# Expert stage in two lanes of 64 rows, each with its own expert, on the two column halves of the array

## What is computed

```
flat = expert.reshape(-1)
counts = jnp.bincount(flat, length=N_EXPERTS)
...
return (jax.nn.silu(xb @ w_eg[e]) * (xb @ w_eu[e])) @ w_ed[e]
...
y = jnp.einsum('nk,nkd->nd', gate.astype(t.dtype), y)
```

## Time and profile before

| | us |
|---|---|
| median of 3 runs | 2869.02 |
| lowest and highest | 2868.82, 2869.57 |
| the profiled execution | 2867.73 |
| its span in the trace | 2866.1 |
| first gate matmul of the expert stage to the first transfer of the stage behind it | 1717.1 to 2818.0 |

### The profile page before, as it was taken

One profiled execution on the slowest core, in us unless ns is written; L12 is line 12 of the kernel. 1 busy time (PEld: TensorE's weight loads), 2 busy tenths in 40 slices (PEclk: granted clock), 3 DMA queues, 4 the chain that ended last, 5 costly groups with the idle time before them and its releaser, 6 DMA issues. The chain is left out here.

```text
span 2866.1 us, 28552 instructions
## 1 busy us (share of the span) xinstructions
PE 2592.7 (90%) x7895; PEld 1293.1 (45%) x7896; DVE 854.1 (30%) x2231; ACT 498.1 (17%) x982; POOL 697.3 (24%) x582
## 2 busy tenths in 40 slices
PE   5797999999995896999999939999999999999990
PEld 2344444444442473455555524444444444444440
DVE  0136665757578111233333330110011010101103
ACT  1121222222211122222222101111111111111112
POOL 0024645555464000011111111111111111211114
PEclk9898999999997998999999969999999999999995
DMA  7120111010104115322111136677756784645966
GB/s 279 59 99 26 42 47 55 33 55 33 59 30 176 54 76 212 117 74 74 59 59 59 59 116 214 193 248 230 261 180 228 244 290 132 223 143 188 340 211 264
DMA packets 153556, 397.15 MB, mean 139 GB/s; under 512 B 18498, under 2 KB 19034, under 8 KB 153482
## 3 DMA queue, kind: packets, MB, share of 16 engines
q1 hardware_dynamic: 125533, 338.28, 32.7%
q0 software_dynamic: 18336, 51.53, 7.5%
q10 hardware_dynamic: 9621, 6.51, 0.8%
HBM read 326.16 MB, written 70.35 MB: 138 GB/s over the span
## 5 line engine op out<-in xcount | busy, mean ns | idle before, releaser
L773 PE MATMUL a_psz<-W 128*128 128x512 f32 x1088 | 484.6, 599 | 1.3 <-ACT W L585 1.3
L671 DVE SCALAR_TENSOR_TENSOR yacc<-aext,pcol,yacc 128x256 f32<-128x256 f32 x928 | 369.9, 477 | 0.0
L1838 PE MATMUL e_psg<-W,e_xT 128*128 x784 | 346.4, 595 | 2.0 <-DVE e_xT L1797 2.0
L1859 PE MATMUL e_psy<-W,e_hT 128*128 x784 | 344.7, 593 | 1.0 <-ACT e_hT L1770 1.0
L1842 PE MATMUL e_psu<-W,e_xT 128*128 x784 | 344.5, 593 | 0.0
L773 PEld LDWEIGHTS a_psz<-W 128*128 128x128 f32 x1088 | 205.7, 193 | 239.2 <-issue 239.2
L555 POOL TENSOR_TENSOR a_vn<-a_vn,gv 128x512 f32<-128x512 f32 x17 | 243.1, 14303 | 15.2 <-ACT a_vn L619 15.2
L1544 PE MATMUL r_psx<-W 128*128 128x512 f32 x544 | 238.1, 596 | 0.0
L1842 PEld LDWEIGHTS e_psu<-W,e_xT 128*128 128x128 f32 x784 | 149.3, 190 | 187.2 <-issue 187.2
L1803 DVE TENSOR_TENSOR e_hb<-e_psu,e_sg 128x512 f32<-128x512 f32 x49 | 33.9, 692 | 661.4 <-PE e_psu L1842 352.8
L1518 PE MATMUL r_pss<-W,r_h2T 128*128 128x512 f32 x512 | 227.5, 598 | 1.4 <-DVE r_h2T L1390 1.4
(11 more groups left out here) (276 smaller groups left out, 2193.1 us busy)
## 6 DMA issues: line engine op xcount, KB each, us to landing
W<-in_w_expert_gate SPq DMA_DIRECT2D x32, 2048.0 KB, 12.9
W<-in_w_expert_up SPq DMA_DIRECT2D x32, 2048.0 KB, 18.2
W<-in_w_expert_down SPq DMA_DIRECT2D x32, 2048.0 KB, 22.4
W<-in_x_prompt SPq DMA_DIRECT2D x32, 512.0 KB, 3.9
x_scratch<-W SPq DMA_DIRECT2D x17, 512.0 KB, 2.9
r_x1r<-x_scratch SPq DMA_DIRECT2D x17, 512.0 KB, 4.3
x_scratch<-r_x SPq DMA_DIRECT2D x17, 512.0 KB, 2.9
h_scratch<-r_h SPq DMA_DIRECT2D x17, 512.0 KB, 2.9
```

Of the source, the lines that this page charges most:

```text
L671: ins = dve.scalar_tensor_tensor(out=out, in0=src, scalar=w, in1=yacc[:, i, :], op0=ALU.mult, op1=ALU.add)
L773: last = pe.matmul(psz[bank][:], hT[t.par][:, k, :], w_in[:, k, COL[bank]:COL[bank] + 512], start=(k == 0), stop=(k == KD - 1))
L1838: last = pe.matmul(psg[:], xT[t.par][:, k, :], W[:, bass.ds(base + 512 * k, 512)], start=(k == 0), stop=(k == KD - 1))
L1859: last = pe.matmul(psy[:, 512 * n:512 * n + 512], hT[:, k, :], W[:, bass.ds(base + 8192 + 1024 * k + 512 * n, 512)], start=(k == 0), stop= ...
```

## The change

The 128 rows of a step become two lanes of 64 rows. Lane 0 works through the experts 0 to 15, lane 1 through the experts 16 to 31, each with blocks of up to 64 pairs of its own expert. Each matmul of 128 rows becomes two of 64 rows (`both`), one into the partitions 0 to 63 of the result and one into 64 to 127, which is on the two column halves of the array. Lane 1 has one slot of `W`, lane 0 the two others by turns; gate, up and down have a semaphore each, and a part of an expert can be loaded as soon as that part of the expert before is done. The order of the loads is sorted on the chip. The planning stage is gone, and its work is done at the start of the expert stage, with the list of steps turned by PE into rows. On PE, a step now ends what it begins: gate_up of this step, then the transposes of the next step's tokens and this step's hidden rows by turns, then down of this step. The bound of the loop is `STEPS_MAX`, 83, where `NBMAX` was 65.

```
-NBMAX = (PAIRS - NE) // P + NE
+LANES = 2
+HALF = P // LANES
+EPL = NE // LANES
+REG = CAP + HALF
+STEPS_MIN = PAIRS // P
+STEPS_MAX = (PAIRS - EPL) // HALF + EPL
...
-        def load_part(eng, e, slot, n):
-            base = W[:, EXPERT_COLS * slot + 4096 * n:EXPERT_COLS * slot + 4096 * n + 4096]
-            name, k, here = (("w_expert_gate", KD, gate_up_here), ("w_expert_up", KD, gate_up_here), ("w_expert_down", KE, down_here))[n]
-            eng.dma_start(base.rearrange("p (k n) -> p k n", k=k),
+        def load_part(eng, e, base, n, r):
+            name, k, here = (("w_expert_gate", KD, gate_here), ("w_expert_up", KD, up_here), ("w_expert_down", KE, down_here))[n]
+            need(eng, here, 16 * r)
+            if not isinstance(r, int):
+                settle(eng)
+            dst = W[:, base + 4096 * n:base + 4096 * n + 4096] if isinstance(base, int) else W[:, bass.ds(base + 4096 * n, 4096)]
+            eng.dma_start(dst.rearrange("p (k n) -> p k n", k=k),
                           I[name][0][bass.ds(e, 1), :, :].rearrange("a (k p) n -> p (a k) n", p=P)).then_inc(here, 16)
-        def load_expert(eng, e, slot):
-            need(eng, gate_up_here, 32 * e)
-            for n in range(2):
-                load_part(eng, e, slot, n)
-            need(eng, down_here, 16 * e)
-            load_part(eng, e, slot, 2)
...
-            def count_blocks(eng):
-                return eng.value_load(ends[0:1, NE - 1:NE], min_val=PAIRS // P, max_val=NBMAX)
-            def block_steps(eng, nb, parts):
+            def count_steps(eng):
+                eng.wait_ge(S["count_known"], 1)
+                return eng.value_load(count[0:1, 0:1], min_val=STEPS_MIN, max_val=STEPS_MAX)
+            def expert_steps(eng, ns, parts):
                 def step(b):
                     for k, work in parts:
                         t = b.at(k)
-                        if isinstance(t.v, int):
-                            if 0 <= t.v < PAIRS // P:
-                                work(t)
-                                continue
-                            if t.v < 0:
-                                continue
-                        with eng.If(t.v < nb):
+                        if isinstance(t.v, int) and t.v < STEPS_MIN:
                             work(t)
-                steps(eng, step, 4, (NBMAX - 3) // 2, NBMAX + 1)
+                            continue
+                        with eng.If(t.v < ns):
+                            work(t)
+                steps(eng, step, 4, (STEPS_MAX - 4) // 2, STEPS_MAX)
...
-                    load_expert(sp, 2, 2)
-                    def load(e, slot):
-                        first = sp.value_load(starts1[0:1, bass.ds(e - 2, 1)], min_val=1, max_val=NBMAX + 1)
-                        sp.wait_ge(S["blocks_left"], first)
-                        load_expert(sp, e, slot)
-                    with sp.Fori(0, (NE - 3) // 6) as g:
-                        for u in range(6):
-                            load(6 * g + (3 + u), u % 3)
-                    for e in range(3 + (NE - 3) // 6 * 6, NE):
-                        load(e, e % 3)
+                    for n in range(3):
+                        load_part(sp, 1, 2 * EXPERT_COLS, n, 2)
+                    sp.wait_ge(S["loads_known"], 1)
+                    with sp.Fori(0, NE - 3) as g:
+                        r = g + 3
+                        free = sp.value_load(loads_row[0:1, 0, bass.ds(r, 1)], min_val=1, max_val=STEPS_MAX + 1)
+                        e = sp.value_load(loads_row[0:1, 1, bass.ds(r, 1)], min_val=0, max_val=NE - 1)
+                        base = sp.value_load(loads_row[0:1, 2, bass.ds(r, 1)], min_val=0, max_val=2 * EXPERT_COLS)
+                        sp.wait_ge(S["gate_done"], free)
+                        settle(sp)
+                        load_part(sp, e, base, 0, r)
+                        sp.wait_ge(S["up_done"], free)
+                        settle(sp)
+                        load_part(sp, e, base, 1, r)
+                        sp.wait_ge(S["down_done"], free)
+                        settle(sp)
+                        load_part(sp, e, base, 2, r)
...
+                    def fetch_pairs(t, dst, here):
+                        for lane in range(LANES):
+                            base = pool.value_load(steps_row[0:1, lane, bass.ds(t.v, 1)], min_val=0, max_val=NE * REG - HALF)
+                            pool.dma_start(dst[HALF * lane:HALF * lane + HALF, :], table_d[bass.ds(base, HALF), :]).then_inc(here, 16)
...
-                    block_steps(pool, nb, [(2, gather), (3, fetch), (0, fetch_again), (-1, scatter)])
+                    ns = count_steps(pool)
+                    expert_steps(pool, ns, [(2, gather), (3, fetch), (0, fetch_again), (0, scatter)])
...
-                    block_steps(act, nb, [(-1, hT_out), (0, silu), (1, xT_out), (-1, y_evac)])
+                    ns = count_steps(act)
+                    expert_steps(act, ns, [(0, silu), (0, hT_out), (1, xT_out), (0, y_evac)])
...
                     def hidden(t):
                         dve.wait_ge(S["silu_done"], t.v + 1)
-                        dve.wait_ge(S["up_psum"], t.v + 1)
-                        need(dve, S["h_turned"], t.v)
-                        dve.tensor_tensor(hb[:], psu[:], sg[:], ALU.mult).then_inc(S["h_done"], 1)
+                        dve.wait_ge(S["up_done"], t.v + 2)
+                        need(dve, S["h_turned"], 2 * t.v)
+                        for m in range(2):
+                            c = slice(256 * m, 256 * m + 256)
+                            dve.tensor_tensor(hb[:, c], psu[:, c], sg[:, c], ALU.mult).then_inc(S["h_done"], 1)
...
+                    expert_steps(dve, ns, [(2, tokens), (0, hidden), (0, hT_out), (1, xT_out), (0, y_evac)])
...
                     def weights(t):
-                        e = pe.value_load(expert_of[0:1, bass.ds(t.v, 1)], min_val=0, max_val=NE - 1)
-                        return e, pe.value_load(slot_base[0:1, bass.ds(e, 1)], min_val=0, max_val=(SLOTS - 1) * EXPERT_COLS)
+                        e = pe.value_load(steps_row[0:1, 2, bass.ds(t.v, 1)], min_val=0, max_val=EPL - 1)
+                        wanted = pe.value_load(steps_row[0:1, 3, bass.ds(t.v, 1)], min_val=16, max_val=16 * NE)
+                        return pe.value_load(slot_base[0:1, bass.ds(e, 1)], min_val=EXPERT_COLS, max_val=2 * EXPERT_COLS), wanted
+                    def both(out, xt, base, at, start, stop):
+                        pe.matmul(out[0:HALF, :], xt[:, 0:HALF], W[:, bass.ds(base + at, 512)], start=start, stop=stop)
+                        return pe.matmul(out[HALF:P, :], xt[:, HALF:P], W[:, at:at + 512], start=start, stop=stop)
...
                     def gate_up(t):
-                        e, base = weights(t)
-                        pe.wait_ge(gate_up_here, 32 * e + 32)
+                        base, wanted = weights(t)
+                        pe.wait_ge(gate_here, wanted)
...
                         for k in range(KD):
-                            last = pe.matmul(psg[:], xT[t.par][:, k, :], W[:, bass.ds(base + 512 * k, 512)], start=(k == 0), stop=(k == KD - 1))
+                            last = both(psg, xT[t.par][:, k, :], base, 512 * k, k == 0, k == KD - 1)
...
                     def down(t):
-                        e, base = weights(t)
-                        pe.wait_ge(down_here, 16 * e + 16)
-                        pe.wait_ge(S["hT_done"], t.v + 1)
+                        base, wanted = weights(t)
+                        pe.wait_ge(down_here, wanted)
+                        if isinstance(t.v, int) and t.v == 0:
+                            pe.wait_ge(S["loads_known"], 1)
                         need(pe, S["y_done"], 2 * t.v)
-                        for n in range(2):
-                            for k in range(KE):
-                                last = pe.matmul(psy[:, 512 * n:512 * n + 512], hT[:, k, :],
-                                                 W[:, bass.ds(base + 8192 + 1024 * k + 512 * n, 512)], start=(k == 0), stop=(k == KE - 1))
-                            last.then_inc(S["blocks_left" if n else "y_psum"], 1)
-                    turn_x(fixed(0))
-                    block_steps(pe, nb, [(-1, turn_h), (0, gate_up), (1, turn_x), (-1, down)])
+                        for m in range(2):
+                            pe.wait_ge(S["hT_hi" if m else "hT_lo"], t.v + 1)
+                            for n in range(2):
+                                for k in (2 * m, 2 * m + 1):
+                                    last = both(psy[:, 512 * n:512 * n + 512], hT[:, k, :], base, 8192 + 1024 * k + 512 * n, k == 0, k == KE - 1)
+                                if m:
+                                    last.then_inc(S["down_done" if n else "y_half"], 1)
...
+                    expert_steps(pe, ns, [(0, gate_up), (1, x_lo), (0, h_lo), (1, x_mid), (0, h_hi), (1, x_hi), (0, down)])
```

(39 more changed lines are left out.)

268 lines of the change are left out of this document (143 added, 125 removed).

## The result

| | us |
|---|---|
| before, median | 2868.92 |
| changed, median of 4 (2915.82 to 2921.05) | 2919.22 |
| ratio, 95% interval | 1.0174 (1.0156 to 1.0192) |
| profiled execution, its span | 2917.70, 2916.1 |

The account below looks back on a forecast made before the run. Only PE was taken to bound the expert stage. 2867.7 + 29.6 (stage with absent steps) - 10.7 (start) = 2886.6, plus 1.3 to the median = 2888, plus 48 (clock) = 2936 us; range 2855 to 3010.

Parts of the forecast that it names:

- the clock: Expert stage: idle array time lowers the clock, two steps in three losing 1.7 us, +48 us; bounds 0 and 143.
- 42 steps, halves side by side: Expert stage: 42 steps in place of 49, two half matmuls at once, 20.61 us a step for the three matrices.
- The fourth rival: Weight loads of 64 columns stand outside the matmuls, 0.14 us each: +564 us, near 3500 us; chance 0.03.
- E to down: From the end of up on the array (E) to the start of down: 4.3 us, making a step 24.91 us.
- The third rival: Value loads at the head of down not exposed: 2783 us; at 0.5 us each, clock 1.00, 2855; chance 0.12.
- The tests behind the last step: Behind the last down part, PE tests twenty absent pairs and one step: 86.7 us in place of 23.4.
- The start: The expert stage's first gate matmul comes at 1706.4 us, 10.7 us sooner; bounds 0 and -14.
- Weights: Expert stage: waits for weight parts add 0 us, up to 30 us in all if short experts end together.
- The sixth rival: Weights come late where lane 1 changes expert each step or two: +30 to +60 us, near 2980; chance 0.06.

## Why the prediction was right

Direction and size held, 2919 for 2936, or +50 for +67. Most of the 17 us are in one term, the clock. By its own steps:

- **42 steps, halves side by side.** Right: gate and up 6.87 us each for both lanes, and the same with one lane left out. The fourth rival fell: a half's load of 0.14 us costs nothing here. With it fell the sentence of the Trainium skill ("TensorE: Matmul & The Clock Gate", Part 3, "Packing small matmuls") that loads overlap matmuls only between row groups. The same section also lets a load into a background weight buffer go ahead of matmuls, which would agree; no run here tells how the load was hidden.
- **E to down.** 4.3 forecast, 4.10 measured in the loop. Hidden rows turned from E + 0.85 (0.74), first value load at E + 1.6 (1.66), three loads 2.27 (2.24); the waits behind are 0.3. The chain of causes is shown: with none, two and three loads ahead of down it begins at 2.03, 2.85 and 3.60. The third rival, on the other side, would have needed the sequencer to go on past a wait. The order alone on blocks of 128 costs 90.7 us.
- **The clock.** Mechanism right, size too large: 48 forecast, 34 measured (20 down parts at 1.7), mean clock of the steps 0.97 for 0.95. The slow start of the first step is there before as well (half speed to 1720.4 before, to 1711.9 now). Filling the idle time gave 33.5 back. I had taken two steps in three, a choice between few rows; it was one in two.
- **The tests behind the last step.** 86.7 forecast (its terms add up to 86.6), 85.3 measured, and the parts held: a pair 4.37 (4.36), the last step 1.3 (1.9), the barrier 0.8 (1.0), the sequencer 4.3 ahead (3.65). Its lead does follow the number of instructions for the same array time, as the prediction has it: it is 7.8 us with one lane's matmuls left out. The end of the last scatter, 10.9 us, lies beside the walk. That the 23.4 us before were all walk was wrong, 13.8 of them stay without one; the sum took them as measured and lost nothing by it. What was missed is what comes next once PE's tests are gone: DVE's five parts a step, 50.5 us, not POOL's.
- **The start.** -10.7 forecast, -8.6 measured. From the plan's first matmul to gate it is 17.6 us in place of 28.6, 11.0 less; but that matmul came 2.4 us later than before, 1.6 of it already there when the router stage began. In the other kernels with lanes gate began between 1707.9 and 1710.1.
- **Weights.** 0 forecast, 1.6 us of waits ahead of gate in all, 0.6 of it for weights (up to 2.8 in the kernels with shorter steps). The sixth rival fell: parts asked for one by one land in 10 to 11 us.

So the account is: from the first gate matmul to the last matmul's end 1073.7 us in place of 1077.5, -3.8, of which the clock is +34 and all else -38; stretch behind the last matmul +62; start -8.6; together 49.5 of the 50. The seven steps that were saved had to pay for the new order and the clock, and little was left of them; the absent steps made the loss. With the exposed loads and the absent steps taken away, the kernel with lanes is 4.9% faster than before, 4.6% where neither has absent steps.

## What to carry to other kernels

A sequencer that stops at a wait late in a step exposes every value load, test and register instruction behind it: count them from that wait on, and load what later parts need ahead of it. In a loop with a bound for the worst case, count tests times absent steps for each engine, and test once around the whole body. A kernel that saves matmuls can lose it all in such places, so look at idle gaps of 2 us with their clock before the count of matmuls.

## What was not expected of the hardware

- The clock against the array's longest idle time in a step, as the runs showed it: 2.16 us, 20 of 38 down parts of the loop with a half-speed stretch; 1.67 us, 8 of 38; 1.37 us (blocks of 128), only the last; 0.9 us, one of 38, in the last step, whose idle time is 1.33; 0.47 and 0.1 us, none. Which part is hit went in a regular pattern, every second one at 2.16 us, every fourth or fifth at 1.67. The length of one idle time does not settle it: the last step's 2.6 us were followed by half speed with the loop ended at 42 and by full speed in the changed kernel.
- A skipped test costs PE 0.20 to 0.21 us for the branch, DVE 0.056 and POOL 0.045 (branches as recorded). Per absent pair, with all around them, that was 4.37 us on PE (14 tests), 2.44 on DVE (10) and 1.78 on POOL (8).
- Two float32 matmuls more, issued ahead of the value loads, delayed down by 0.04 us only.

Not tried: down one step later with the lanes, as in the order before; so what the lanes are worth without the new order is not shown. SP waits for down's end between the loads of one expert and the next, and gate of the next step may need the next one.
